# Identity multiplications on TensorE around the norms of a two-model forward pass

## The chip, the cores and the metric

The kernel runs on one core of a Trainium2 chip. The metric is the device time of one execution in microseconds (us). TensorE's clock is granted at one of two levels, 2.4 GHz (shown as 1.00) and 1.2 GHz (shown as 0.50).

## What is computed

The input is 256 tokens of width 1024, in float32. A first block of four layers and a second one of two layers follow each other:

```python
def rms_norm(x, g):
    xf = x.astype(jnp.float32)
    y = xf * lax.rsqrt(jnp.mean(xf * xf, axis=-1, keepdims=True) + EPS)
    return (y * g.astype(jnp.float32)).astype(x.dtype)

def swiglu(x, w_gate_up, w_down):
    g, u = jnp.split(x @ w_gate_up, 2, axis=-1)
    return (jax.nn.silu(g) * u) @ w_down
...
    for i in range(DEPTH):
        h = h + 0.5 * swiglu(rms_norm(h, norm_ffn1[i]), ffn1_w_gate_up[i], ffn1_w_down[i])
        hn = rms_norm(h, norm_mix[i])
        kind, j = i % N_MIXERS, i // N_MIXERS
        ...
        h = h + mix
        h = h + 0.5 * swiglu(rms_norm(h, norm_ffn2[i]), ffn2_w_gate_up[i], ffn2_w_down[i])
    return rms_norm(h, final_norm)
```

The mixers are three kinds of attention (stick-breaking, block attention, latent attention). Each of the second block's two layers is a norm, a mixer of three parts (differential attention, gated linear attention, short convolution), a norm, and a product-key lookup (`peer`) that gathers 128 rows for each token from each of two tables of 16384 rows.

## The kernel before, in words

The program is a list of phases, `plan()`, that all engines walk in the same order. Each engine has its own in-order instruction stream; semaphores (`S[...]`) tie them together. The phases with their starts on TensorE in the trace: a norm before the feed-forward (`ffn`) at 26 us, then norms at 225, 372, 569, 766, 929, 1124, 1319, 1473, 1667, 1863 and 2010 us, each followed by the next feed-forward or mixer; at 2204 us `norm_final`, in which TensorE has nothing to do, and right behind it the norm at 2213 us; then the norms at 2409 us (before the first lookup), 3118 us and 3315 us (before the second lookup). So there are 16 norms with work for TensorE, and the final norm of all without.

A norm works on two tiles of 128 tokens (`t`) with two halves of 512 columns each. ScalarE squares and sums the rows (L1098), VectorE forms the mean (L1530), GpSimd its power of -1/2 (L2152), and VectorE scales (`xn`, L1507) and counts `normed` for each half. TensorE transposes each half in four 128x128 pieces into one of four PSUM banks `work` (L737), 16 transposes in all. In a `norm_split` phase ScalarE copies each transposed group into `x_hi` (L1112), VectorE subtracts it to get `x_lo` (L1523), and after four groups the next phase begins; in a plain `norm` (before the latent attention and the two mixers of the second block) ScalarE (L1067) and VectorE (L1389) copy the groups to `xT`.

In `ffn`, `sb`, `moba` and `peer` a product of float32 values is made as three products of hi and lo parts (`split_mm`, L645 to L647). The weights come by DMA into `wide_ring` and `deep_ring`, ScalarE rounds them (`wide_hi`, L1142) and VectorE forms the rest (`wide_lo`, L1396). Each half panel is 16 `split_mm`, so 48 matmuls with 256 columns on TensorE. A phase ends with products into the four banks `acc`, which VectorE adds to `resid` (L1544): the first 128 tokens while TensorE still works on the second.

The norm on TensorE is the function below. Its last two waits are for the four groups to have left the banks.

Of the kernel before, what the change touches and what calls it, by code (L numbers as in the profile page):

```python
# [25 lines left out]
P = 128  # L26
# [93 lines left out]
def panels_of(kind):  # L120
# [11 lines left out]
    if kind == "pq":  # L132
# [10 lines left out]
                 moved_odd=2, gains=1),  # L143
    "norm_split": dict(square_sum=2, mean_square=2, rstd=2, normed=4, turned=4, moved_even=2,
                     moved_odd=2, gains=1, x_hi=4),
# [8 lines left out]
                 moved_odd=4, scores=HEADS, masked=HEADS, row_max=HEADS, exps=HEADS,  # L154
                 probs=HEADS, probs_T=HEADS, weights=HEADS, mixed=HEADS, mixed_read=HEADS),
    "mla": dict(wide=18, wide_read=18, deep=4, half_deep=1, resid=4, rotated=3, mean_square=1, rstd=1,
                turned=20, moved_even=10, moved_odd=10,
# [3 lines left out]
                 turned=10, moved_even=5, moved_odd=5,  # L161
# [6 lines left out]
def plan():  # L168
    phases = []
    for i in range(DEPTH):  # L170
        phases += [Phase("norm_split", gain=("norm_ffn1", i)), Phase("ffn", which=1, i=i),
                   Phase("norm" if i % 3 == 2 else "norm_split", gain=("norm_mix", i)),
                   Phase(("sb", "moba", "mla")[i % 3], i=i, j=i // 3),
                   Phase("norm_split", gain=("norm_ffn2", i)), Phase("ffn", which=2, i=i)]
    phases.append(Phase("norm_final", gain=("final_norm", None), last=False))
    for i in range(DEPTH2):
        phases += [Phase("norm", gain=("norm_mix_2", i)), Phase("mix2", i=i),
                   Phase("norm_split", gain=("norm_ffn_2", i)), Phase("peer", i=i)]
    phases.append(Phase("norm_final", gain=("norm_final_2", None), last=True))
    total = {}  # L180
    for n, ph in enumerate(phases):
        ph.n = n
        ph.at = dict(total)
        for name, count in RAISES[ph.kind].items():
            total[name] = total.get(name, 0) + count
    return phases


def build(nc, A, out, stop=None):
    phases = plan()[:stop]  # L190
    ctx = ExitStack()
    with ctx:
        def sb(name, shape, dt=F32):
            return ctx.enter_context(nc.sbuf_tensor(name, shape, dt))

        def sem(name):
            return ctx.enter_context(nc.semaphore(name))
# [24 lines left out]
        def cut(at, *shape):  # L222
# [67 lines left out]
        ident = sb("ident", [P, P])  # L290
# [46 lines left out]
        acc = [[bank[0], bank[1]], [bank[2], bank[3]]]  # L337
        work = bank[4:8]


        S = {name: sem(name) for name in (
            "square_sum",
            "mean_square",
            "rstd",
            "normed",
            "turned",
            "moved_even",
            "moved_odd",
            "x_hi",
# [55 lines left out]
        def seen(count):  # L405

            return max(count, 0)
# [122 lines left out]
        wide_dmas, n = [], [0] * GSLOTS  # L530
        for ph in phases:
            for k in range(RAISES[ph.kind].get("wide", 0) // 2):
                g = ph.at.get("wide", 0) // 2 + k
# [19 lines left out]
        def _(sp):  # L553
# [18 lines left out]
            def panel(ph, k):  # L572
                w, kt, _, c0, n, _ = panels(ph)[k]
                load_wide(ph, k, lambda slot: [(wide_ring[:, slot, 0:kt, 0:n],
                                                w.rearrange("(k p) n -> p k n", p=P)[:, :, c0:c0 + n])])
# [53 lines left out]
        def _(pe):  # L629
            mm = nc.tensor.matmul  # L630
# [87 lines left out]
            def turn_groups(ph, first, groups):  # L718

                for g, tiles in enumerate(groups):  # L720
# [5 lines left out]
                                                  src, ident[:])  # L726
                    ins.then_inc(S["turned"], 1)

            def norm(ph):
                for t in range(TT):  # L730
                    for half in range(2):
                        pe.wait_ge(S["normed"], ph.at.get("normed", 0) + 2 * t + half + 1)
                        g = ph.at.get("turned", 0) + 2 * t + half
                        pe.wait_ge(S["moved_even" if g % 2 == 0 else "moved_odd"], seen((g - 4) // 2 + 1))
                        for i in range(4):
                            c = 4 * half + i
                            ins = nc.tensor.transpose(work[g % 4][:, i * P:(i + 1) * P],  # L737
                                                      xn[:, t, c * P:(c + 1) * P], ident[:])
                        ins.then_inc(S["turned"], 1)
                pe.wait_ge(S["moved_even"], ph.at.get("moved_even", 0) + 2)  # L740
                pe.wait_ge(S["moved_odd"], ph.at.get("moved_odd", 0) + 2)

# [312 lines left out]
            for ph in phases:  # L1055
                {"norm": norm, "norm_split": norm, "norm_final": lambda ph: None, "ffn": ffn, "sb": stick_breaking,
                 "moba": block_attention, "mla": latent_attention, "mix2": parallel_mixer,
                 "peer": product_keys}[ph.kind](ph)
# [325 lines left out]
        def _(dve):  # L1384
# [35 lines left out]
            def latent_projections(ph):  # L1420

                for k, (_, _, _, c0, n, layout) in enumerate(panels(ph)):
                    if ph.kind == "mla" and k == 2:
                        latent_norms(ph)
                    for j in range(2):
                        t = ph.at["wide"] + 2 * k + j
                        dve.wait_ge(S["wide"], t + 1)
                        b = work[t % 4]
                        if ph.kind == "mla":
                            if k < 2:  # L1430
                                dst = ml_c[:, j, c0:c0 + n]
                            elif k < 5:
                                dst = ml_q[:, j].rearrange("p h d -> p (h d)")[:, (k - 2) * 512:(k - 1) * 512]
                            else:

                                h0 = 4 * (k - 5)
                                s = b[:, :].rearrange("p (h x) -> p h x", h=4)
                                V.tensor_copy(ml_k[:, j, h0:h0 + 4, 0:64], s[:, :, 0:64])
                                V.tensor_copy(ml_v[:, j, h0 * 64:(h0 + 4) * 64].rearrange(
                                    "p (h x) -> p h x", h=4), s[:, :, 64:128]).then_inc(S["wide_read"], 1)  # L1440
                                continue
                        V.tensor_copy(dst, b[:, 0:n]).then_inc(S["wide_read"], 1)
# [777 lines left out]
```

## Time and profile before

| | us |
|---|---|
| median of 3 runs | 4037.35 |
| the runs | 4033.81, 4037.35, 4037.63 |
| the profiled execution, its own time | 4033.32 |
| its span, first to last instruction | 4031.6 |
| TensorE busy (matmul) | 3063.5 (76%) |
| VectorE, ScalarE, GpSimd busy | 2523.8, 1118.4, 1033.3 |
| mean granted clock of TensorE | 0.887 |

Busy time is summed over the whole span; what limits a stretch must be read in that stretch. In the timelines each row is a run of like instructions: its start, its length, and in brackets how long the engine had been idle and what released it. Matmuls overlap, so the pace of a row is told by the distance of starts, not by the length of one.

### The profile page before, as it was taken

What the parts mean: (1) busy time and instruction counts of PE and PEld (TensorE: products, weight loads), DVE (VectorE), ACT (ScalarE), POOL (GpSimd) and SP (SyncE); (2) the same over time, 40 slices, a digit from 0 to 9 for tenths busy, and PEclk for the clock granted to TensorE, in tenths of its full rate; (3) what the DMA queues carried; (4) which work ended last, traced back from release to release, by engine and by line L of the source; (5) the groups of instructions that cost most, each with busy time, mean ns of one, the idle gap of its engine ahead of it and who ended that gap; (6) DMA issues with size and microseconds to landing.
All of it is one profiled execution on the core that took longest, in us unless ns stands there. A gap on an engine that the chain in (4) does not pass through costs nothing.

```text
span 4031.6 us, 45300 instructions
## 1 busy us (share of the span) xinstructions
PE 3063.5 (76%) x17118; PEld 2387.5 (59%) x17118; DVE 2523.8 (63%) x4415; ACT 1118.4 (28%) x1545; POOL 1033.3 (26%) x1110
## 2 busy tenths in 40 slices
PE   7999999979999789999999966343435966343434
PEld 6997989968989469899698645111112645111111
DVE  4555454555555455555555258988886259988886
ACT  3334333333333133333433222111110222111110
POOL 0000000000000000000000006777775006777775
PEclk9999999999999899999999978777778978776778
DMA  5543545614556135555246227999999327999998
GB/s 176 187 162 110 186 164 188 222 43 163 183 168 210 55 121 183 186 184 197 95 143 206 107 89 293 409 409 409 409 409 356 145 89 296 409 409 409 409 409 334
DMA packets 415040, 940.91 MB, mean 233 GB/s; under 512 B 27888, under 2 KB 210192, under 8 KB 414864
## 3 DMA queue, kind: packets, MB, share of 16 engines
q0 software_dynamic: 150048, 546.37, 34.3%
q1 hardware_dynamic: 259744, 390.09, 28.6%
q10 hardware_dynamic: 5072, 2.12, 0.2%
q8 instruction: 107, 1.75, 0.2%
q14 instruction: 69, 0.57, 0.0%
HBM read 937.45 MB, written 1.05 MB: 233 GB/s over the span
## 4 chain that ended last, share of the span: by engine, by line
PE 58%; DVE 20%; DMA 11%; issue 5%; POOL 4%; ACT 1%; ACTq 1%; DVEq 0%; SPq 0%; POOLq 0%
PE pair L645 14%; PE pair L646 14%; PE pair L647 14%; DVE wide_ring L2001 7%; DMA wide_ring<-in_peer_u,pk_idx 5%; PE pair L689 4%; PE pair L710 4%; POOL wide_ring L2173 3%; DMA deep_ring<-in_peer_v,pk_idx 2%; DMA wide_ring<-in_peer_v,pk_idx 2%; DVE deep_ring L2001 2%; DMA deep_ring<-in_peer_u,pk_idx 2%; DVE pair L2041 1%; PE pair L695 1%; DVE xn L1507 1%
## 5 line engine op out<-in xcount | busy, mean ns | idle before, releaser
L645 PE MATMUL pair<-x_hi,wide_hi 128*128 128x256 f32 x3328 | 952.0, 286 | 22.5 <-DVE x_lo L1523 20.0
L646 PE MATMUL pair<-x_lo,wide_hi 128*128 128x256 f32 x3328 | 948.9, 285 | 0.0
L647 PE MATMUL pair<-x_hi,wide_lo 128*128 128x256 f32 x3328 | 948.7, 285 | 0.0
L1049 PE MATMUL pair<-wide_ring,arena 128*128 128x512 f32 x816 | 435.9, 672 | 593.0 <-DMA wide_ring<-in_peer_v,pk_idx 502.5
L1396 DVE TENSOR_TENSOR wide_lo<-wide_ring,wide_hi 128x2048 fp32r<-128x2048 f32 x228 | 522.0, 2289 | 486.4 <-ACT wide_hi L1142 486.2
L2152 POOL TENSOR_TENSOR small<-small,minus_half 128x1 f32<-128x1 f32 (+2 forms) x41 | 27.5, 672 | 2616.3 <-DVE small L1530 2282.5
L1049 PEld LDWEIGHTS pair<-wide_ring,arena 128*128 128x128 f32 x816 | 161.2, 214 | 865.7 <-issue 749.9
L645 PEld LDWEIGHTS pair<-x_hi,wide_hi 128*128 128x128 f32 x3328 | 646.4, 194 | 31.5 <-DVE x_lo L1523 24.0
L646 PEld LDWEIGHTS pair<-x_lo,wide_hi 128*128 128x128 f32 x3328 | 646.5, 194 | 2.6
L647 PEld LDWEIGHTS pair<-x_hi,wide_lo 128*128 128x128 f32 x3328 | 646.0, 194 | 0.0
L1142 ACT ACTIVATE wide_hi<-wide_ring 128x2048 fp32r<-128x2048 f32 x228 | 435.9, 1912 | 489.8 <-DMA wide_ring<-in_ffn_w_gate_up 323.6
L2001 DVE CUSTOM_DVE_ANT_0 wide_ring<-wide_ring,pair 128x1024 f32<-128x1024 f32 x408 | 493.4, 1211 | 24.3 <-DMA wide_ring<-in_peer_u,pk_idx 22.1
L2173 POOL DMA_INDIRECT wide_ring<-in_peer_u,pk_idx x408 | 394.1, 966 | 131.3 <-issue 102.5
L2173 POOL DMA_INDIRECT wide_ring<-in_peer_v,pk_idx x408 | 392.4, 962 | 127.1 <-issue 96.4
L1374 ACT ACTIVATE arena<-ident,pk_coef 128x128 f32<-128x128 f32 x256 | 78.2, 388 | 767.4 <-DVE pk_coef L2016 767.4
L2041 DVE SCALAR_TENSOR_TENSOR pair<-wide_ring,pk_coef,pair 128x1024 f32<-128x1024 f32 x176 | 226.8, 1289 | 88.7 <-DMA wide_ring<-in_peer_v,pk_idx 73.2
L645 PE MATMUL pair<-deep_hi,hid_hi 128*128 128x512 f32 x640 | 250.0, 391 | 0.0
L646 PE MATMUL pair<-deep_lo,hid_hi 128*128 128x512 f32 x640 | 250.0, 391 | 0.0
L647 PE MATMUL pair<-deep_hi,hid_lo 128*128 128x512 f32 x640 | 249.0, 389 | 0.0
L1049 PE MATMUL pair<-deep_ring,arena 128*128 128x512 f32 x208 | 112.6, 674 | 145.4 <-DMA deep_ring<-in_peer_v,pk_idx 145.3
L1560 DVE TENSOR_TENSOR xn<-pair,xn 128x256 f32<-128x256 f32 x176 | 74.3, 422 | 227.8 <-ACT xn L1156 227.8
L1581 DVE TENSOR_TENSOR deep_lo<-deep_ring,deep_hi 128x2048 fp32r<-128x2048 f32 x80 | 183.2, 2290 | 25.3 <-ACT deep_hi L1172 23.3
(291 smaller groups left out, 4380.3 us busy)
## 6 DMA issues: line engine op xcount, KB each, us to landing
wide_ring<-in_ffn_w_gate_up SPq DMA_DIRECT2D x176, 1024.0 KB, 9.5
deep_ring<-in_ffn_w_down SPq DMA_DIRECT2D x88, 1024.0 KB, 5.0
wide_ring<-in_sb_w_qkv SPq DMA_DIRECT2D x12, 2048.0 KB, 12.3
wide_ring<-in_w_in SPq DMA_DIRECT2D x12, 2048.0 KB, 9.8
wide_ring<-in_peer_w_q SPq DMA_DIRECT2D x8, 2048.0 KB, 12.4
wide_ring<-in_moba_w_qkv SPq DMA_DIRECT2D x6, 2048.0 KB, 12.2
deep_ring<-in_sb_w_o SPq DMA_DIRECT2D x8, 1024.0 KB, 8.2
deep_ring<-in_w_out SPq DMA_DIRECT2D x8, 1024.0 KB, 8.1
```

What stands on the lines that cost most here:

```text
L645: mm(o, w[0], x[0], start=start, stop=False, skip_group_check=True)
L646: mm(o, w[0], x[1], start=False, stop=False, skip_group_check=True)
L647: return mm(o, w[1], x[0], start=False, stop=stop, skip_group_check=True)
L689: ins = mm(b[:, 0:n], src[:, c, j * P:(j + 1) * P], w[:, c, 0:n], start=c == 0, stop=c == kt - 1)
L710: ins = mm(acc[t][h][:, :], lhs(c)[:, t * P:(t + 1) * P], w[:, c, h * 512:(h + 1) * 512], start=k == 0 and c == 0, stop=last and c == 1, s ...
L1049: ins = mm(acc[t][h][:, :], pk_diag[:, s % 2, k], row_at(ph, row)[:, h * 512:(h + 1) * 512], start=first, stop=last, skip_group_check=True)
L1142: A_(wide_hi[:, split_at(ph, j)], half_panel(ph, wide_ring[:, g % GSLOTS], j), ACT.Copy).then_inc(S["wide_hi"], 1)
L1396: V.tensor_tensor(wide_lo[:, split_at(ph, j)], half_panel(ph, wide_ring[:, slot], j), wide_hi[:, split_at(ph, j)].bitcast(F32), ALU.subtra ...
L1581: V.tensor_tensor(lo, deep_ring[:, slot], hi.bitcast(F32), ALU.subtract).then_inc(S["deep_lo"], 1)
L2001: V.tensor_tensor_reduce(out=row_at(ph, row), in0=row_at(ph, row), in1=pair[1 + s // PK_HEADS][:], scale=1.0, scalar=0.0, op0=ALU.mult, op ...
L2041: V.scalar_tensor_tensor(out=total, in0=row_at(ph, row), scalar=coef, in1=total, op0=ALU.mult, op1=ALU.add).then_inc(S["row_used"], 1)
L2173: G.indirect_dma_start(row_at(ph, k), None, tables[table], bass.IndirectOffsetOnAxis(ap=pk_idx[:, s, n:n + 1], axis=0)).then_inc(row_in[sl ...
```

## The change

A helper `keep_busy(b, n)` multiplies the identity by itself n times, into the first 128 columns of a PSUM bank. In each norm it runs ahead of the transposes: 9 times in general, 38 times where the phase before is `norm_final`, 5 times where it is the lookup, not at all in the first norm. The bank is the one that the last of the four groups of transposes will overwrite. It runs again behind the transposes, 6 times, into the first bank of `acc`, which the next phase overwrites. Behind a mixer of the second block TensorE first waits until all five groups of each parity that the mixer transposed have been moved. Results are not used. VectorE's, ScalarE's, GpSimd's and the DMA queues' instructions stay as they are.

```diff
+            def keep_busy(b, n):
+
+                for _ in range(n):
+                    mm(b[:, 0:P], ident[:], ident[:], start=True, stop=True, skip_group_check=True)
+
             def norm(ph):
+                if ph.n > 0:
+                    before = phases[ph.n - 1].kind
+                    if before == "mix2":
+                        pe.wait_ge(S["moved_even"], phases[ph.n - 1].at["moved_even"] + 5)
+                        pe.wait_ge(S["moved_odd"], phases[ph.n - 1].at["moved_odd"] + 5)
+                    g = ph.at.get("turned", 0) + 3
+                    keep_busy(work[g % 4], {"norm_final": 38, "peer": 5}.get(before, 9))
                 for t in range(TT):
                     for half in range(2):
...
                         ins.then_inc(S["turned"], 1)
+                keep_busy(acc[0][0], 6)
                 pe.wait_ge(S["moved_even"], ph.at.get("moved_even", 0) + 2)
                 pe.wait_ge(S["moved_odd"], ph.at.get("moved_odd", 0) + 2)
```

## Rows read from the trace of the kernel before

**Rows 1.** The page, busy time and slices; digits are tenths.

```profile
PE 3063.5 (76%) x17118; PEld 2387.5 (59%) x17118; DVE 2523.8 (63%) x4415; ACT 1118.4 (28%) x1545; POOL 1033.3 (26%) x1110
...
PEclk9999999999999899999999978777778978776778
```

**Rows 2.** Waits of TensorE in one feed-forward, 372 to 569 us: total, times, longest.

```profile
PE pair L737 <- DVE xn L1507: 2.9, 2, 2.0
PE pair L645 <- DVE x_lo L1523: 1.5, 1, 1.5
```

**Rows 3.** TensorE's timeline at the norm at 225 us: start, length, instructions [idle before].

```profile
222.67 0.39 PE L647 MATMUL pair<-wide_hi,hid_lo 128*128 128x512 f32 x1
225.10 1.32 PE L737 MATMUL pair<-ident,xn 128*128 128x128 f32 x8 [2.04 <-DVE xn L1507]
227.25 1.97 PE L737 MATMUL pair<-ident,xn 128*128 128x128 f32 x8 [0.82 <-DVE xn L1507]
```

**Rows 4.** TensorE's timeline behind it.

```profile
230.67 0.55 PE L645 MATMUL pair<-x_hi,wide_hi 128*128 128x256 f32 x1 [1.46 <-DVE x_lo L1523]
231.02 0.41 PE L646 MATMUL pair<-x_lo,wide_hi 128*128 128x256 f32 x1
231.24 0.41 PE L647 MATMUL pair<-x_hi,wide_lo 128*128 128x256 f32 x1
...
233.86 0.28 PE L645 MATMUL pair<-x_hi,wide_hi 128*128 128x256 f32 x1
233.98 0.28 PE L646 MATMUL pair<-x_lo,wide_hi 128*128 128x256 f32 x1
```

**Rows 5.** Stretches there: us, busy (instructions) by engine, granted clock, DMA.

```profile
223.10:226.80 3.70, 1.31 (x8) 0.84 (x8) 3.04 (x7) 2.09 (x4) 1.49 (x3) 1.00 0.98 358
226.80:230.60 3.80, 1.97 (x8) 1.57 (x8) 3.61 (x6) 2.20 (x4) 0.17 (x1) 0.50 0.44 137
230.60:233.70 3.10, 3.03 (x14) 3.06 (x15) 2.02 (x1) 1.04 (x1) 0.00 (x0) 0.51 0.00 1
```

**Rows 6.** VectorE's and ScalarE's timelines at that norm.

```profile
227.77 1.95 DVE L1523 TENSOR_TENSOR x_lo<-pair,x_hi 128x512 fp32r<-128x512 f32 x3
...
225.80 1.26 ACT L1112 ACTIVATE x_hi<-pair 128x512 fp32r<-128x512 f32 x2 [0.22 <-PE pair L737]
```

**Rows 7.** TensorE's timeline at the norm at 1473 us.

```profile
1473.15 1.32 PE L737 MATMUL pair<-ident,xn 128*128 128x128 f32 x8 [2.04 <-DVE xn L1507]
1475.30 1.32 PE L737 MATMUL pair<-ident,xn 128*128 128x128 f32 x8 [0.82 <-DVE xn L1507]
1478.40 0.35 PE L645 MATMUL pair<-x_hi,wide_hi 128*128 128x256 f32 x1 [1.78 <-DVE x_lo L1523]
```

**Rows 8.** TensorE's timeline at its first norm.

```profile
28.39 1.97 PE L737 MATMUL pair<-ident,xn 128*128 128x128 f32 x8 [0.16 <-DVE xn L1507]
33.69 0.55 PE L645 MATMUL pair<-x_hi,wide_hi 128*128 128x256 f32 x1 [3.34 <-DVE x_lo L1523]
```

**Rows 9.** Stretches behind the norms at 372 and 3315 us (first and last of seven).

```profile
377.70:383.80 6.10, 6.10 (x28) 6.10 (x29) 2.29 (x1) 2.25 (x2) 0.00 (x0) 0.50 0.71 240
...
3320.30:3326.10 5.80, 5.74 (x27) 5.77 (x28) 2.29 (x1) 1.96 (x2) 0.00 (x0) 0.50 0.09 33
```

**Rows 10.** TensorE's timeline at the norm at 929 us.

```profile
929.51 1.78 PE L737 MATMUL pair<-ident,xn 128*128 128x128 f32 x8 [2.04 <-DVE xn L1507]
931.65 1.92 PE L737 MATMUL pair<-ident,xn 128*128 128x128 f32 x8 [0.36 <-DVE xn L1507]
```

**Rows 11.** TensorE's timeline, eight passes of four float32 products with 128 columns.

```profile
2423.06 1.16 PE L1024 MATMUL pair<-pk_keysT,arena 128*128 128x128 f32 x8 [0.69 <-ACT arena L1340]
```

**Rows 12.** TensorE's timeline at norms behind other phases and before a plain one.

```profile
1323.58 1.10 PE L689 MATMUL pair<-wide_ring,xT 128*128 128x512 f32 x2 [0.83 <-issue]
...
2213.51 1.97 PE L737 MATMUL pair<-ident,xn 128*128 128x128 f32 x8 [8.98 <-DVE xn L1507]
...
3117.63 1.78 PE L737 MATMUL pair<-ident,xn 128*128 128x128 f32 x8 [2.95 <-DVE xn L1507]
```

**Rows 13.** Stretches with many small matmuls, and with transposes alone.

```profile
305.00:312.00 7.00, 5.21 (x44) 4.69 (x43) 5.26 (x11) 6.17 (x14) 0.00 (x0) 1.00 0.01 2
...
766.10:769.50 3.40, 3.17 (x14) 2.77 (x15) 2.74 (x6) 1.77 (x5) 1.08 (x2) 0.51 0.71 249
769.50:771.30 1.80, 0.41 (x3) 0.17 (x2) 1.77 (x3) 1.76 (x3) 0.00 (x0) 0.99 0.43 150
```

**Rows 14.** Waits of TensorE behind the norm at 2409 us.

```profile
PE pair L645 <- DVE wide_lo L1396: 1.1, 1, 1.1
```

## Prediction

> **What bounds the kernel now.** I read the page first, then the waits of single phases, then the timelines at the norms. TensorE is busy for 3063.5 of 4031.6 us, and the row of granted clock sits at 9 tenths, not 10, through the part where it is busiest [rows 1]. So there is time at the low level inside the first 2200 us. The waits of one whole feed-forward, 372 to 569 us, show that TensorE waits only at the norm ahead of it, 2.9 us for `xn` and 1.5 us for `x_lo`, and never for weights, ScalarE or VectorE afterwards [rows 2]. A feed-forward is thus bound by TensorE, and whatever its matmuls lose or win at the start of a phase reaches the phase's end.
>
> The norm at 225 us shows what is lost. The phase before ends with a matmul that starts at 222.67; TensorE stands still for 2.04 us, transposes eight pieces in 1.32 us, waits 0.82, and transposes eight more, which now take 1.97 us [rows 3]. Over 223.1 to 226.8 us it was busy for 1.31 us at a granted clock of 1.00; from 226.8 to 233.7 us the clock is 0.50 [rows 5]. The next phase starts its products at 230.67 us, and while the clock is low they start every 0.213 us (231.02 to 231.24), after that every 0.12 us (233.86 to 233.98) [rows 4]. So each microsecond of dense products at the low level holds 0.12 / 0.213 = 0.563 us of work; 0.437 us of it are lost.
>
> The norm at 1473 us is the one whose clock did not fall: both groups of eight take 1.32 us, and dense work at the high level starts 1478.40 - 1473.15 = 5.25 us after the first transpose [rows 7], against 230.67 - 225.10 = 5.57 us at 225 us [rows 3, 4]. The low clock costs 0.32 us there, since the transposes of the second token tile end later and `x_hi` and `x_lo` with them.
>
> **What the change adds.** A product of two float32 operands is two passes in the trace: four products of 128 columns are eight instructions and last 1.16 us at the high clock, of which the last one is 0.28 and the rest give 0.11 to 0.12 us a pass [rows 11]. An identity product is the same shape, so 0.22 us, and at the low clock 2 x 0.213 = 0.43 us (the low pace of a 256-column pass of the split products is also that of the transposes of 128 columns: eight in 1.97 us, less a tail of 0.42 and a slower first one).
>
> - Nine ahead of the transposes: 9 x 0.22 = 1.98 us. They can issue about 0.23 us after the last matmul's start, at 222.9, and end issuing at about 224.9; the transposes start at 225.10 [rows 3]. They lie in the idle 2.04 us, cost nothing, and if they run over by 0.1 or 0.2 us ScalarE's wait of 0.22 us ahead of `x_hi` [rows 6] grows, and the second tile's transposes, which wait for VectorE until 227.25, do not move.
> - Six behind them: 6 x 0.22 = 1.32 us at the high clock. The last transpose then starts about 1.05 us after 227.25 and the six end at about 229.7; the products would start at 230.67 - 0.32 = 230.35 us. They are hidden by VectorE's four `x_lo`, the first three of which alone take 1.95 us [rows 6]. At the low clock they take 12 x 0.213 = 2.56 us and would not be hidden.
> - Behind `norm_final`: 38 x 0.22 = 8.4 us into 8.98 us idle; behind the lookup 5 x 0.22 = 1.1 us into 2.95 us [rows 12]. Both hidden at the high clock.
> - In the three plain norms the room behind the transposes is only 0.83 us plus the tail of the last one [rows 12]. At 1319 us, with everything high, the six end at about 1320.88 + 1.05 + 0.11 + 1.32 = 1323.36 us, and the first product now starts at 1323.58: a gain of 0.2 us where a gain of 0.55 would be had without the six. At 2213 and 3118 us it comes out at zero.
> - The added wait behind a mixer is for moves that the mixer's last products, which follow later in the same stream, leave far behind: nothing.
>
> **What it takes away.** If TensorE is never idle for long around a norm, the clock should not fall. With the fillers the 7.6 us between two dense phases hold 1.98 + 1.32 + 1.32 + 1.32 = 5.9 us of work. The trace has a stretch with a like density: in the stick-breaking attention, 305 to 312 us, TensorE is busy for 5.21 of 7.0 us in small pieces, and the clock stays at 1.00 [rows 13]. The lone norm that held, at 1473 us, did so with 2.64 us of transposes alone [rows 7], so the norms are at the edge even without help. I take it that all of them hold.
>
> The dense stretches at the low level that then go: 33.69 to 39.0 us in the first phase (5.3 us, at the pace of rows 4), 3.0 us at 230.67 [rows 5], and seven more from 6.1 us behind 377.7 to 5.8 us behind 3320.4, with 3.3, 3.4, 3.3, 2.9 and 3.3 us between them [rows 9]. The sum is 5.3 + 3.0 + 6.1 + 3.3 + 3.4 + 3.3 + 2.9 + 3.3 + 5.8 = 36.4 us, and 0.437 of it is **15.9 us**. The first norm belongs here although it gets only the six behind: they turn 2.56 of its 3.34 idle us [rows 8] into work, so TensorE is dense from 28.4 us on and the clock should rise some 5 us sooner.
>
> The late starts that go: 7 norms like that at 225 us x 0.32 = 2.2 us; at 766, 929 and 1124 us, where the low level covered only the transposes (1.78 and 1.92 us instead of 1.32 [rows 10]), 0.1, 0.27 and 0.16 us; at 1319 us 0.2 us. Together **2.9 us**. The whole sum is 18.8 us: the profiled execution, 4033.3 us by its own time, would take 4014.5 us.
>
> Against the median: that execution was 4.0 us below the median of 4037.35 us. Where the clock falls and comes back differs from one execution to the next, so part of that distance is the very loss that goes, and another part stays. I keep 1.5 us: **4016 us**, 0.53% faster. A measurement of this kernel can tell about 0.2% (8 us) from no change.
>
> **A rule against it.** At 766 us the clock was low while TensorE did 14 transposes in 3.40 us and nothing else, and it was 0.99 in the stretch right after, which has only three instructions [rows 13]. So here transposes raise the clock like other matmuls. The Trainium skill ("TensorE: Matmul & The Clock Gate", Part 4: PE-mode transpose) says the opposite, that transposes do not count as TensorE being busy; by it the chip would see nothing between the nine and the six. The trace does not agree with it; it is the second rival below, with what it would do here.
>
> **Rivals.**
>
> 1. *The clock holds, but the gain is partly taken back.* In the lookup phases TensorE meets VectorE: behind the norm at 2409 us it waits 1.1 us for `wide_lo` [rows 14], so the 0.437 x (3.3 + 5.8) = 4.0 us gained there may vanish into longer waits. If two or three other norms still fall as well (2 us each) and the first phase gains half of its 2.3, the sum is 18.8 - 4.0 - 5 - 1.2, about 8.6 us: 4027 us. For it speaks that phases of attention have waits of their own; against it that the products at their heads are dense.
>
> 2. *The transposes do not hold the clock, and the six stand in the way.* Between the nine's end at 224.9 and the six's start at 228.4 there are 3.5 us with transposes alone. Should the clock fall there, the second tile's transposes run as now, and the six behind them start at about 229.0 and take 2.56 us, to 231.6: 0.9 us later than the 230.67 at which the next phase starts now [rows 4]. The place is TensorE's in-order stream, since the next phase's products are queued behind the six. At 13 norms that is 12 us, and the losses of now stay: 4037 + 12 = 4049 us. It decides as soon as the six run at the low clock, since 2.56 us is more than the 1.46 us of idle time plus the tail of the last transpose. Against it: the clock came back after transposes alone [rows 13], and it held at 1473 us [rows 7].
>
> 3. *The change does not do what it says.* The clock falls as often as before, since it goes by something other than these products, but the six mostly run before it falls. All is hidden: 4037 us.
>
> **How the numbers follow.** The forecast has 0.80, with 4011 to 4022 us of its own (from no offset and a first phase that gains more, to an offset of 4 us and two norms that still fall). Rival 1 has 0.09, rival 2 has 0.06 and rival 3 has 0.05. The range that holds 8 in 10 reaches into rival 1: 4010 to 4028 us. Faster by over 0.2% (below 4029.3) is the forecast and rival 1: 0.89; within 0.2% is rival 3: 0.05; slower is rival 2: 0.06.
>
> **What would show it.** Right: the granted clock is 1.00 in the stretches around all norms but the first, both groups of eight transposes take 1.32 us everywhere, the products of the next phase start every 0.12 us from the first on, and 18 passes of the new line stand in the idle 2.04 us. Some 36 us of dense work and 50 us within the norms are then no longer at 0.50, so the mean clock of the profile rises by (36 + 50) / 2 / 4030, about 0.01. Wrong: transposes of 1.97 us behind the nine, or a first product that waits for the six and not for `x_lo`. If an identity product costs more than 0.23 us, the nine delay the first transposes.

## The result, and the profile after

The changed kernel takes 4015.0 us (median of 5 runs, 4013.2 to 4015.6) against 4037.35 us (median of 5, 4029.4 to 4040.5): the ratio is 0.9948, with an interval of 0.9933 to 0.9962. The forecast was 4016 us, with 4010 to 4028 us as the range. The profiled execution took 4013.2 us by its own time, 20.1 us less than the one of before; the sum said 18.8.

At the norm at 224 us, the one of [rows 3] and [rows 4], TensorE's timeline of the changed kernel reads:

```profile
221.37 0.39 PE L647 MATMUL pair<-wide_hi,hid_lo 128*128 128x512 f32 x1
221.60 2.17 PE L732 MATMUL pair<-ident 128*128 128x128 f32 x18
223.80 1.32 PE L749 MATMUL pair<-ident,xn 128*128 128x128 f32 x8
225.94 1.32 PE L749 MATMUL pair<-ident,xn 128*128 128x128 f32 x8 [0.82 <-DVE xn L1520]
227.09 1.50 PE L732 MATMUL pair<-ident 128*128 128x128 f32 x12
229.04 0.36 PE L645 MATMUL pair<-x_hi,wide_hi 128*128 128x256 f32 x1 [0.45 <-issue]
229.23 0.28 PE L646 MATMUL pair<-x_lo,wide_hi 128*128 128x256 f32 x1
229.35 0.28 PE L647 MATMUL pair<-x_hi,wide_lo 128*128 128x256 f32 x1
```

Line 732 is `keep_busy`, 749 the transposes. The nine products are 18 passes of 2.17 us and end where the 2.04 us of idle time ended. Both groups of transposes take 1.32 us. The six end 0.45 us before the first product, which starts as long behind the first transpose as it did at 1473 us without fillers, where it waited for `x_lo` [rows 7]. The products of the next phase start every 0.12 us from the second on. From the first transpose to the first product it is 5.24 us (5.57 before). The 12 norms that follow a product phase and stand ahead of split products look like this, with 5.24 to 5.26 us from the first transpose to the first product. The clock in the windows around them (columns as in [rows 5]) has no stretch at 0.50:

```profile
223.80:229.00 5.20, 3.97 (x28) 3.06 (x28) 4.48 (x8) 3.97 (x7) 1.11 (x2) 1.00 0.62 213
229.00:239.50 10.50, 10.46 (x87) 10.49 (x88) 5.28 (x3) 2.61 (x2) 0.00 (x0) 1.00 0.01 2
369.10:384.00 14.90, 13.59 (x109) 12.69 (x109) 8.90 (x13) 8.19 (x10) 1.09 (x2) 1.00 0.68 242
```

The last of them covers what answers to the first of [rows 9]. At the first norm, which gets only the six, the clock was back when they began, and the products behind the remaining pause start every 0.12 us (0.213 before, [rows 8] and [rows 4]):

```profile
31.21 1.50 PE L732 MATMUL pair<-ident 128*128 128x128 f32 x12
34.77 0.36 PE L645 MATMUL pair<-x_hi,wide_hi 128*128 128x256 f32 x1 [2.06 <-DVE x_lo L1536]
```

At one norm the clock fell, the one behind the first lookup, which gets five products:

```profile
3098.28 1.28 PE L732 MATMUL pair<-ident 128*128 128x128 f32 x10
3101.39 1.32 PE L749 MATMUL pair<-ident,xn 128*128 128x128 f32 x8 [1.84 <-DVE xn L1520]
3103.53 1.97 PE L749 MATMUL pair<-ident,xn 128*128 128x128 f32 x8 [0.82 <-DVE xn L1520]
3105.29 2.13 PE L732 MATMUL pair<-ident 128*128 128x128 f32 x12
3107.26 1.03 PE L695 MATMUL pair<-xT,wide_ring 128*128 128x256 f32 x4
```

Here 1.84 us stay idle, the second group runs low, and the six end right at the next product. The waits of the feed-forward of [rows 2] shrink to 0.8 and 0.4 us:

```profile
PE pair L749 <- DVE xn L1520: 0.8, 1, 0.8
PE pair L645 <- issue: 0.4, 1, 0.4
```

To see where the 20.1 us are, take the distance of the first transposes of one norm from those of the next as the length of a phase (in us; the last one runs to the end of the span):

| phase | before | after | forecast gain | gain |
|---|---|---|---|---|
| ffn at 26 | 198.8 | 196.4 | 2.3 | 2.4 |
| sb at 225 | 147.0 | 145.4 | 1.6 | 1.7 |
| ffn at 372 | 197.4 | 194.3 | 3.0 | 3.1 |
| ffn at 569 | 196.5 | 194.3 | 1.8 | 2.2 |
| moba at 766 | 163.5 | 163.6 | 0.1 | -0.1 |
| ffn at 929 and 1124 | 389.2 | 388.9 | 0.4 | 0.4 |
| mla at 1319 | 154.4 | 154.8 | 0.2 | -0.4 |
| ffn at 1473 | 194.3 | 194.3 | 0.0 | 0.0 |
| ffn at 1667 | 195.8 | 194.3 | 1.5 | 1.5 |
| sb at 1863 | 147.2 | 145.4 | 1.8 | 1.8 |
| ffn at 2010, norm_final | 203.2 | 201.3 | 1.6 | 1.9 |
| mix2 at 2213 | 195.9 | 194.3 | 0.0 | 1.6 |
| peer at 2409 | 708.3 | 706.9 | 1.8 | 1.4 |
| mix2 at 3118 | 197.2 | 197.4 | 0.0 | -0.3 |
| peer at 3315 | 716.8 | 712.7 | 2.8 | 4.1 |

Against the sum of 21.2 us stands a start that was 1.1 us later: the first transposes begin at 27.37 us, not 26.29. Nothing of the change comes before them, and in the traces below they begin anywhere from 26.3 to 27.9 us.

### The profile page after: what moved, and what is told of

Same layout as the page of the kernel before. It is cut to its first block, busy times and chain, and to the rows that moved or that the text cites. A ratio compares the mean times of both kernels' runs of the same rounds, so it can differ in the third digit from the quotient of the medians.

```text
span 4011.5 us, 46326 instructions
## 1 busy us (share of the span) xinstructions
PE 3099.4 (77%) x17630; PEld 2423.3 (60%) x17630; DVE 2521.4 (63%) x4415; ACT 1118.7 (28%) x1545; POOL 1034.9 (26%) x1110
## 4 chain that ended last, share of the span: by engine, by line
PE 59%; DVE 19%; DMA 11%; issue 5%; POOL 4%; ACT 1%; ACTq 1%; DVEq 0%; POOLq 0%
PE pair L645 14%; PE pair L646 14%; PE pair L647 14%; DVE wide_ring L2014 7%; DMA wide_ring<-in_peer_u,pk_idx 5%; PE pair L689 4%; PE pair L710 4%; POOL wide_ring L2186 3%; DMA deep_ring<-in_peer_v,pk_idx 2%; DMA wide_ring<-in_peer_v,pk_idx 2%; DVE deep_ring L2014 2%; DMA deep_ring<-in_peer_u,pk_idx 2%; DVE pair L2054 2%; PE pair L695 1%; DVE xn L1520 1%
## 5 line engine op out<-in xcount | busy, mean ns | idle before, releaser
L645 PEld LDWEIGHTS pair<-x_hi,wide_hi 128*128 128x128 f32 x3328 | 638.2, 192 | 15.7 <-DVE x_lo L1536 8.9
L646 PEld LDWEIGHTS pair<-x_lo,wide_hi 128*128 128x128 f32 x3328 | 638.3, 192 | 2.6
```

The source lines that it names most:

```text
L645: mm(o, w[0], x[0], start=start, stop=False, skip_group_check=True)
L646: mm(o, w[0], x[1], start=False, stop=False, skip_group_check=True)
```

## The experiments

They ran on other chips, on which the kernel before takes 4179 to 4192 us. The traces show where that comes from: a lookup phase lasts 774 to 792 us there instead of 707 to 717, and in the kernel before the other phases are within 3 us of those above. So ratios to the kernel before on the same chip are compared, and the phases around norms one by one.

**Only the products ahead.**

```diff
-                keep_busy(acc[0][0], 6)
```

> The identity products behind the transposes are left out, those ahead of them stay (9, 38 or 5). The theory (the change saves time only by keeping TensorE's clock at 2.4 GHz across a norm): with 1.32 + 0.82 + 1.32 us of transposes and then 1.8 us idle, the clock still falls at most norms, mostly later than before, during or behind the transposes, so the dense products still start low. Expected: most of the gain is gone, 4028 to 4038 us, the stretches behind most norms at 0.50 again. Rival (each half fills its own gap and brings its share, nine against six): about 4023 us. Rival (the gain has to do with the first group of transposes, which follow the nine directly): near 4015 us.

Measured: 4183.6 against 4190.5 us, ratio 0.9983 (0.9974 to 0.9993), so 7 us of gain. The timeline at 225 us, and stretches of dense products at the low level behind two norms:

```profile
225.48 1.32 PE L749 MATMUL pair<-ident,xn 128*128 128x128 f32 x8
227.63 1.31 PE L749 MATMUL pair<-ident,xn 128*128 128x128 f32 x8 [0.82 <-DVE xn L1519]
230.73 0.55 PE L645 MATMUL pair<-x_hi,wide_hi 128*128 128x256 f32 x1 [1.79 <-DVE x_lo L1535]
```

```profile
230.30:233.80 3.50, 3.07 (x14) 3.10 (x15) 2.62 (x2) 1.07 (x1) 0.00 (x0) 0.51 0.00 0
1124.60:1131.50 6.90, 5.99 (x28) 6.02 (x29) 3.10 (x3) 1.56 (x1) 0.00 (x0) 0.51 1.06 370
```

Both groups of transposes run high, and then the clock falls around the 1.79 us of idle time behind them, as the dense work starts. So it is at nine of the 16 norms of this trace; at a tenth, the one behind the first lookup, it falls under the second group. The theory holds; the shares by number (nine of fifteen) do not: they ask for 4023 us or 0.9965, outside the interval.

**Only the products behind.** The block under `if ph.n > 0:` is left out.

> The identity products ahead of the transposes and the added wait are left out, the six behind stay. Theory: 2.04 us idle, then transposes and six products without a long pause; the clock falls at some norms, and where it has fallen it comes back by the time dense work starts, but then the six run at 0.213 us a pass and end up to 0.9 us late. Expected: 4017 to 4024 us, few dense stretches at 0.50, first products late by 0 to 0.9 us where the six ran low. Rival (shares by number): about 4028 us.

Measured: 4173.2 us, ratio 0.9958 (0.9941 to 0.9975), 17 us of gain. In this trace the clock fell at every norm but the first, mostly under the transposes:

```profile
222.78 1.32 PE L742 MATMUL pair<-ident,xn 128*128 128x128 f32 x8 [2.04 <-DVE xn L1513]
224.92 1.97 PE L742 MATMUL pair<-ident,xn 128*128 128x128 f32 x8 [0.82 <-DVE xn L1513]
226.67 2.77 PE L732 MATMUL pair<-ident 128*128 128x128 f32 x12
229.09 0.56 PE L645 MATMUL pair<-x_hi,wide_hi 128*128 128x256 f32 x1
```

```profile
224.20:231.00 6.80, 6.08 (x29) 6.09 (x30) 5.53 (x7) 3.52 (x4) 0.44 (x1) 0.50 0.23 83
229.10:231.00 1.90, 1.90 (x11) 1.90 (x11) 1.65 (x1) 0.21 (x1) 0.00 (x0) 0.50 0.00 0
```

The six run low, 2.77 us, and the next product follows with no idle time. The low level ends 1.9 us into the dense products here, and before them at 11 of the 15 norms at which it fell. The second half of the change carries most of the gain, because it is the dense phase that pays for a low clock. The first half lets the six themselves run high; the feed-forwards take 194.4 to 195.3 us here and 194.3 with both halves. What it adds to the whole time is small: 0.9958 is within its interval of the 0.9948 and 0.9952 of the whole change.

**Transposes as fillers.**

```diff
-                    mm(b[:, 0:P], ident[:], ident[:], start=True, stop=True, skip_group_check=True)
+                    nc.tensor.transpose(b[:, 0:P], ident[:], ident[:])
```

with twice as many of them.

> Every identity product is replaced by two transposes of the identity (18, 76 or 10 ahead, 12 behind), so that between two dense phases TensorE does nothing but transposes; a transpose is one pass, so the passes are as many as in the change. If transposes count for the clock like products: 4015 us as the change, granted clock 1.00 around the norms. If they do not count, as the Trainium skill says (TensorE: Matmul & The Clock Gate, Part 4: PE-mode transpose): the clock falls at every norm, as there are then 7.6 us without any other matmul, and the 12 transposes behind run low and hold up the next phase by 0.9 us at 13 norms: 4045 to 4055 us.

Measured: 4164.1 us, ratio 0.9938 (0.9921 to 0.9954), as good as the change (0.9952 on the chip of the next group). From the last product of one phase to the first of the next TensorE did nothing but transposes, and the clock stood at 1.00:

```profile
222.15:229.59 7.44, 6.05 (x48) 4.90 (x46) 6.62 (x12) 4.72 (x8) 1.67 (x3) 1.00 0.69 262
```

So transposes of float32 hold the clock as products do, and the second rival loses its ground. The Trainium skill ("TensorE: Matmul & The Clock Gate", Part 4: PE-mode transpose) says that the full clock does not engage for transposes, since they do not count as the engine being busy in the same way. This trace does not agree for float32, by the 1.00 over 7.44 us; no run here has transposes of another type.

**Twelve behind, instead of six.**

> 12 identity products instead of 6 behind the transposes; all else as the change. It measures what fillers cost where nothing hides them. At the high clock they take 24 x 0.111 = 2.66 us instead of 1.33. The changed kernel has 0.45 us idle between the six and the first product, so 0.9 us more at each of 11 norms before split products, 1.3 us at the 3 plain ones and 0 to 0.6 us at the first: 12 to 15 us in all, 4027 to 4031 us. Rival (the stretch behind the transposes is not on the path, for instance since wide_lo is what the next phase waits for): 4015 us.

Measured: 4176.1 us, ratio 0.997 (0.9959 to 0.998). That is 0.0018 worse than the change's 0.9952, some 7 us where 12 to 15 were expected, with intervals nearly as wide. In the trace the feed-forwards take 194.9 or 195.4 us instead of 194.3:

```profile
570.69 2.84 PE L732 MATMUL pair<-ident 128*128 128x128 f32 x24
573.29 0.36 PE L645 MATMUL pair<-x_hi,wide_hi 128*128 128x256 f32 x1
```

The first product starts 2.60 us after the first filler, against 1.95 us (227.09 to 229.04) with six. The price at a norm is 0.65 us and not the 0.9 expected. I had taken the 0.45 us of idle time for all the room, but it is counted from the modelled end of the last pass. The last pass of the six starts 0.72 us before the first product, and here the first product starts 0.03 us after the last pass has started, so the room was about 0.7 us. The stretch is on the path; only the size was off.

**Eighteen ahead, instead of nine.**

```diff
-                    keep_busy(work[g % 4], {"norm_final": 38, "peer": 5}.get(before, 9))
+                    keep_busy(work[g % 4], {"norm_final": 38, "peer": 5}.get(before, 18))
```

> 18 identity products instead of 9 ahead of the transposes (38 and 5 stay). It measures the cost of fillers ahead of the transposes where nothing hides them: 18 more passes of 0.111 us, 2.0 us. The first token tile's transposes start 2.0 us late, but the second tile's wait for VectorE until 2.14 us after the first and so move by at most about 1.1 us (8 transposes behind the late start, less the 0.82 us of idle time), or not at all. Theory: 0.3 to 1.2 us at each of 13 norms, 4 to 15 us over the change. Rival (first transposes are on the path one for one): 2.0 us at each of 13 norms, 26 us over the change, so slower than the kernel before.

Measured: 4160.7 us, ratio 0.996 (0.9945 to 0.9976), beside 4155.7 us for the change on the same chip:

```profile
564.09 4.18 PE L732 MATMUL pair<-ident 128*128 128x128 f32 x36
568.11 1.91 PE L749 MATMUL pair<-ident,xn 128*128 128x128 f32 x16
569.86 1.50 PE L732 MATMUL pair<-ident 128*128 128x128 f32 x12
571.96 0.35 PE L645 MATMUL pair<-x_hi,wide_hi 128*128 128x256 f32 x1 [0.60 <-issue]
```

Two more microseconds ahead make the next product 0.4 us later (the feed-forwards take 194.7 to 195.4 us instead of 194.3). The first token tile's transposes have slack up to the second tile's, so the nine are not as tight as they look. The medians differ by 5 us, which is 12 norms of 0.4 us and lies in the expected 4 to 15; the two intervals overlap. The rival of one for one (26 us) falls.

**Zeros for the identity.** The operands are `zeros_tok[:, 0:P]` twice, and TensorE waits for the constants once.

> The fillers multiply a block of zeros by zeros instead of the identity by itself; TensorE also waits once, before its first phase, for the constants. If the clock goes by what instructions TensorE runs and not by their data: as the change, 0.993 to 0.996 of the kernel before, clock 1.00 around the norms. If data of zeros counts as no work: as without fillers, the clock falls at most norms and the six behind run low, at or above the kernel before.

Measured: 4155.0 us, ratio 0.9944 (0.9929 to 0.9959); the change beside it 4155.7 us. The row of the first product is that of the change:

```profile
226.99 1.50 PE L732 MATMUL pair<-zeros_tok 128*128 128x128 f32 x12
228.94 0.36 PE L645 MATMUL pair<-x_hi,wide_hi 128*128 128x256 f32 x1 [0.44 <-issue]
```

Zeros do as well as the identity, so the gain does not hang on what the operands hold, as far as these two tell.

**The change once more.**

> The changed kernel once more, beside the others of this call on one chip. Theory: 0.993 to 0.996 of the kernel before, as first measured (0.9948).

Measured: 4155.7 against 4179.1 us, ratio 0.9952 (0.9938 to 0.9966).

**Without the 38 and the 5.**

> The 38 identity products behind norm_final and the 5 behind each lookup are left out, all else as the change. Theory: at these three plain norms no dense split products follow the transposes, and the clock is back by the time the first fp32 products run or falls only over the transposes; so leaving them out costs at most 0.3 to 1 us a norm: 0 to 3 us over the change, ratio to the kernel before 0.995 to 0.996. Rival (each filler brings its share, and the 38 are most of one norm's): 3 to 6 us of the gain lost, ratio 0.9965 or more.

Measured: 4167.9 against 4192.4 us, ratio 0.9935 (0.992 to 0.995), not above the 0.995 to 0.996 expected. The ratio shows no loss. Behind `norm_final` the clock is low during all transposes and part of the six, and the plain products that follow start high. Behind the first lookup the six run low throughout, and the low level reaches into the products:

```profile
2200.74 1.97 PE L749 MATMUL pair<-ident,xn 128*128 128x128 f32 x8 [8.62 <-DVE xn L1520]
2202.89 1.97 PE L749 MATMUL pair<-ident,xn 128*128 128x128 f32 x8 [0.17 <-DVE xn L1520]
2204.64 2.06 PE L732 MATMUL pair<-ident 128*128 128x128 f32 x12
2206.54 1.68 PE L695 MATMUL pair<-xT,wide_ring 128*128 128x256 f32 x7
```

```profile
3184.62 2.77 PE L732 MATMUL pair<-ident 128*128 128x128 f32 x12
```

Behind `norm_final` it is 5.80 us from the first transpose to the first product with the clock low and 4.64 us (2200.25 to 2204.89) with the 38: 1.2 us. The phase behind the lookup takes 200.4 us in this trace, and 195.7 to 198.6 us in all others. So the 38 and the 5 may be worth some 1 to 3 us, which is below what the ratio can tell.

**The kernel before once more.**

> The kernel before once more, for its trace on another chip and with the clock falling at other moments. Theory: a feed-forward phase, from its norm's first transpose to the next norm's, takes 194.3 us where the clock held or came back in time and up to 197.4 us where it did not, as in the first trace (194.3, 194.5, 194.8, 195.8, 196.5, 197.4 us); other phases than in the first trace are the slow ones. If instead the slow ones are the same phases as before, the loss belongs to the phase and not to the moment at which the clock falls.

Measured: 4193.0 us, ratio 1.0 (0.9988 to 1.0012). The feed-forwards take 198.2, 196.1, 197.6, 197.0, 197.3, 195.8 and 195.9 us in the order of the table (the last feed-forward apart), where the first trace had 198.8, 197.4, 196.5, 194.8, 194.5, 194.3 and 195.8. The norm of [rows 10], whose dense products ran high in the first trace, makes its phase 2.7 us longer than 194.3 here:

```profile
934.52 1.97 PE L737 MATMUL pair<-ident,xn 128*128 128x128 f32 x8 [0.37 <-DVE xn L1507]
937.95 0.55 PE L645 MATMUL pair<-x_hi,wide_hi 128*128 128x256 f32 x1 [1.46 <-DVE x_lo L1523]
```

```profile
937.90:943.10 5.20, 5.15 (x24) 5.18 (x25) 2.29 (x1) 2.30 (x2) 0.00 (x0) 0.50 0.84 287
```

So the loss belongs to the moment at which the clock falls, not to a phase: four of the seven phases changed by 1.3 to 2.8 us, in both directions.

**More of the same, in the mixers.**

```diff
                     if ph.kind == "mla" and k == 2:
+                        keep_busy(acc[0][0], 32)
...
-                    keep_busy(work[g % 4], {"norm_final": 38, "peer": 5}.get(before, 9))
+                    keep_busy(work[g % 4], {"norm_final": 38, "peer": 12}.get(before, 9))
...
-                keep_busy(acc[0][0], 6)
+                keep_busy(acc[0][0], 3 if ph.kind == "norm" else 6)
...
+                keep_busy(acc[0][0], 23)
...
+                keep_busy(acc[0][0], 26)
...
+                keep_busy(acc[0][0], 33)
```

The 23 stand behind the split products of the block attention, the 26 behind the products of the latent attention, the 33 ahead of the wait for `rotated` + 2 in the second block's mixer.

> The change, and more of it where the changed kernel's trace still shows the clock at 0.50 behind a pause of TensorE: 23 identity products ahead of the transposes of the block attention (5.3 us idle in the changed kernel), 32 and 26 ahead of the two groups of transposes of the latent attention (7.4 and 6.0 us idle), 33 ahead of the last transposes of the second block's mixers (7.75 us idle), 12 instead of 5 behind the lookup, and 3 instead of 6 behind the transposes of the plain norms. Theory: the clock is held there too; the transposes and products behind run at twice the pace, about 3 us in the block attention, 3 + 5 in the latent one, 2 in each of the second block's mixers, 2 us from the rest: 15 us less than the change, ratio to the kernel before 0.991. Rival (in the mixers ScalarE and VectorE set the pace, so a faster TensorE waits longer for them): within 5 us of the change, ratio 0.994 to 0.995.

Measured: 4141.8 against 4179.1 us, ratio 0.9915 (0.9901 to 0.9928), 13.9 us below the change on the same chip: the lowest ratio of this study. In the latent attention the change runs its first ten transposes low, with this version they run high. First the changed kernel's row, then this one's:

```profile
1340.19 2.40 PE L725 MATMUL pair<-ident,arena 128*128 128x128 f32 x10 [7.44 <-DVE small L1743]
```

```profile
1329.82 6.86 PE L733 MATMUL pair<-ident 128*128 128x128 f32 x60
1336.98 1.31 PE L726 MATMUL pair<-ident,arena 128*128 128x128 f32 x10 [0.29 <-DVE small L1747]
```

The phases: latent attention 155.1 to 148.7 us, block attention 160.6 to 159.1, the second block's mixers 194.1 to 194.3 and 196.6 to 195.7. So the expectation of 15 us came out by its total and not by its parts, which is in part luck. The latent attention gave 6.4 of 8 us; the block attention half of 3; in the mixers of the second block it came out as the rival had it. These differences sum to about 8.6 us, and the two profiled executions differ by 7.5 us (4152.2 and 4144.7), the medians by 13.9. The rest is how executions of one kernel differ: the profiled ones lie 3.6 us below and 2.9 us above their medians.

## Why the prediction was right

**The bound.** One reading for it was wrong: in the page's row of the clock 9 is the highest digit there is (90% or more), so "9 tenths, not 10" shows nothing. What shows time at the low level in the first 2400 us is the mean of 0.96 in the window below. That a feed-forward carries a loss at its head through to its end was right: 3.1 us gained for 3.0 forecast at 372 us, 0.0 for 0.0 at 1473 us.

**The fillers.** A pass of 0.11 us was right (18 in 2.17 us, of which 0.27 are the tail); the nine end 0.03 us before the transposes, and the run with 18 shows that another 2 us would cost 0.4. The six were forecast to leave 0.65 us of room, and the run with twelve puts it at about 1.33 - 0.65 = 0.7 us. In the plain norm at 1319 us the first product was to come 2.48 us after the second group begins; it comes 2.50 us after (1312.35 to 1314.85). The 0.2 us were won at the head, yet the phase became 0.4 us longer, and why is not shown. The norm at 3118 us was read wrong: its first product waited 1.68 us for a weight transfer and not 0.83 us.

**What goes away.** The forecast was 15.9 us of dense time and 2.9 us of late starts: in the rows of the table with a forecast above zero, 19.9 us were gained where 18.8 were forecast. The first norm was right by its gain (2.4 us for 2.3) and not by its way: the six were to run low for 2.56 us and bring the clock back, but it was back when they began, and they took 1.50 us. In the other traces with products there the clock was back by 29.7 to 33.6 us, in the three without them not before 38.6 us, so the products do matter, here by keeping the clock and not by bringing it back. The step that was mis-sized is the last lookup, 4.1 us instead of 2.8. Its first gather starts after 24.9 us instead of 27.7 from the first transposes, which is the 2.8; the other 1.3 us come in the 680 us of gathers behind it, and what made them is not shown. GpSimd's timelines, before and after, with the first transposes at 3314.79 and 3298.80:

```profile
3342.52 2.81 POOL L2173 DMA_INDIRECT deep_ring<-in_peer_u,pk_idx  x1 [25.87 <-DVE pk_idx L1981]
```

```profile
3323.68 2.82 POOL L2186 DMA_INDIRECT deep_ring<-in_peer_u,pk_idx  x1 [23.03 <-DVE pk_idx L1994]
```

**What the sum did not have.** The mixer at 2213 us gained 1.6 us where zero was forecast. Inside it there is a stretch of dense plain products that ran low; it is in the kernel before and after, with a different part of it low:

```profile
2281.70:2291.90 10.20, 10.20 (x37) 8.21 (x37) 0.00 (x0) 0.00 (x0) 0.00 (x0) 0.50 0.01 2
```

```profile
2270.30:2280.50 10.20, 10.20 (x29) 6.22 (x29) 0.00 (x0) 0.00 (x0) 0.00 (x0) 0.67 0.00 0
```

With the same code there this phase took 194.1, 197.3 and 197.8 us in three traces with fillers, so its gain here need not be the change's. The same holds for the 1.7 us of the first stick-breaking phase: 145.4 us here, 145.4 to 149.6 us in the other traces with fillers, beside 147.0 and 148.2 us in the two of the kernel before. The later start of the first transposes, 1.1 us, took back most of what the mixer gave. That the sum came within 1.3 us of the profiled execution is in part luck.

**"All of them hold"** was wrong at one norm, behind the lookup: five products leave 1.84 us idle. Its first product comes 0.2 us later than before (5.86 instead of 5.66 us behind the first transpose). The zero forecast at 2213 us, behind `norm_final`, came out at the norm itself: 4.61 us before, 4.64 after.

One argument for the holding was weak. It was that the clock stays at 1.00 in the attention at 305 to 312 us, where TensorE is busy for 5.21 of 7.0 us [rows 13]. In seven of the nine other traces with fillers the clock fell at about that place of the phase, for 6.8 to 10.2 us, and there the phase took 147.5 to 149.6 us. In the trace of the change once more:

```profile
302.90:309.90 7.00, 6.26 (x29) 5.40 (x28) 3.10 (x6) 4.32 (x9) 0.00 (x0) 0.50 0.00 0
```

So that stretch did not show that such work keeps the clock. What shows it for the norms is that the 12 between product phases and split products held here and in every trace with both nine (or eighteen) ahead and six (or twelve) behind.

**The mean clock** was to rise by 0.01 and rose by half of that, from 0.887 to 0.892. The forecast counted 86 us less at the low level. Ahead of the lookups it was 65 us less, and behind them 15 us more, which the forecast did not have; what made the 15 is not shown. The windows of before, then of after, split at the first lookup's norm:

```profile
39.10:2409.40 2370.30, 2224.66 (x14528) 1956.11 (x14526) 1226.27 (x1710) 842.59 (x971) 26.18 (x43) 0.96 0.45 153
2409.40:4031.60 1622.20, 829.51 (x2552) 422.78 (x2552) 1287.67 (x2694) 265.11 (x563) 999.31 (x1036) 0.77 0.89 350
```

```profile
31.00:2394.50 2363.50, 2259.49 (x15001) 1992.16 (x14999) 1230.27 (x1716) 846.65 (x975) 26.18 (x43) 0.98 0.46 154
2394.50:4011.50 1617.00, 836.47 (x2616) 428.02 (x2616) 1287.15 (x2694) 265.21 (x563) 1000.88 (x1036) 0.76 0.89 351
```

**The offset to the median** of 1.5 us was 1.8. The reason given for it has weak support. The five runs of the kernel before spread over 11.1 us, those of the changed one over 2.4 us, which fits a loss that depends on when the clock falls; but on the chip of the run once more it was 11.9 us (nine runs) and 8.9 us (five).

**The rivals.** The first (the gain given back in the lookups) fell: their heads passed it on. The second fell by the run with transposes alone, and its mechanism, six products at the low clock in front of the next phase, could be seen in the run with the six alone (2.77 us, no idle time left), where it costs less than the clock's earlier return is worth. The third fell by the clock's rows.

## What to carry to other kernels

Where TensorE pauses for 2 us or so between dense phases, look at the pace of the first products behind the pause, not at the pause: here 2.9 to 6.1 us of them ran at 0.213 instead of 0.12 us. Work without use in the pause cost nothing here as long as it ended before the wait did, and it mattered most right ahead of the dense work (0.9958 with the six alone, 0.9983 with the nine alone). Size it by passes at the high clock from the trace, and do not expect a gain where another engine sets the pace of what follows.

## What the runs showed of the hardware

Transposes of float32 and products of zeros held the granted clock as the identity products did: 7.44 us of transposes alone at 1.00, and a ratio of 0.9944 with zeros. The same kernel took 4037 us on one chip and 4179 to 4192 us on three others, with nearly all of the difference in the two lookup phases: in the slices of the page the DMA engines moved 409 GB/s on the first chip and mostly 350 to 370 on the others.
